# Splitting weights three pieces ahead of their products instead of two, in a two-block transformer kernel on one core

## The chip, the core and the metric

The kernel runs on one core of a Trainium2 chip. The core has TensorE (PE), which multiplies matrices into PSUM banks, VectorE (DVE), ScalarE (ACT), GpSimd (POOL) and SyncE (SP), which issues the DMAs of the weights here. Each engine works through its own list of instructions in order and waits on semaphores for the others. The metric is the device time of one execution in microseconds, as the median over runs.

## The reference

The input is 256 tokens of width 2048. Two blocks follow each other, all in float32.

```python
# block 1
h = rms_norm(x, pre_norm_w)
proj = h @ w_in                 # q, k, v, z, b, a of the delta rule; q, k, v, z of MoBA; two gates
oa = gated_delta_rule(conv+silu of q, k, v; beta, g)    # 8 heads of 128, chunks of 64
ob = moba_attention(qb, kb, vb)                          # 8 heads of 128, causal
merged = sigmoid(gate_a) * (norm(oa)*silu(z) @ w_branch_a) + sigmoid(gate_b) * (ob*silu(z) @ w_branch_b)
x = x + rms_norm(merged @ w_out, post_norm_w)
# block 2
proj = rms_norm(x, norm_g) @ w_in_2
# a: rope; compressed keys and values: silu(blocks @ cmp_w1) @ cmp_w2; compressed, selected
#    and window attention (8 heads of 128, 2 for keys), mixed by gates, times silu(za)
# b: rope; banded attention, window 128, with a sink per head (16 heads of 64, 2 for keys), times silu(zb)
x = x + concat(y_a, y_b) @ w_out_2
out = rms_norm(x, final_g)
```

## The kernel before

**Pieces and ticks.** All weights pass through the core once, as 398 pieces of 512 KB (fewer bytes for the pieces of kvb), in the order of the list `PIECES`. The program counts in ticks: tick n is the one in which TensorE multiplies piece n. The large products keep float32 accuracy by splitting both factors into a high and a low part; a piece takes part in three products, hi·hi, lo of the weight, and lo of the activations.

**What is done to a piece.** SyncE loads it into one of five raw slots (`load`, L772). ScalarE copies it, rounded, to a high part (`hi_w`, L973), VectorE subtracts this from the raw piece and writes the low part (`lo_w`, L1356). The two share one of four split slots. `split(no)` on ScalarE waits for the load of the piece and for the product of the piece that used the slot before, four full pieces earlier; on VectorE it waits for the high part. TensorE's `products(no)` (L2017 and others) waits for the low part. `load(no)` waits until the raw slot is free: for the lo_w of piece no-5.

**Pieces without a split.** The compression weights are multiplied raw (L1981, the "cmp" kind). They come in turns of two, pieces 276/277, 284/285, 292/293, 300/301, 308/309, 316/317, 324/325 and 332/333; `FULL` is the list of all other pieces. A load whose raw slot holds such a piece waits for TensorE's use of it in place of a lo_w. So load(c+5), with c the first piece of a turn, waits for the product of piece c.

**The order by hand.** `PLAN`, made by `plan()`, holds for each tick the small steps that run beside the products: on each of ScalarE and VectorE, the loop over ticks first splits the piece that `split_at(tick)` names, two full pieces ahead, and then runs the tick's steps. TensorE does the product of the tick first and then its steps. Around the border between the blocks (`BORDER` = 255, the last piece of w_out) `split_at` gives nothing and the splits stand in `PLAN`; also for the last piece (`FINAL` = 397).

**Steps that matter here.** A tile of attention, `att(kind, h, t, n)`, takes five ticks, one for each n: n = 0, the scores on TensorE; n = 1, mask and maximum on VectorE (L1614 to L1622); n = 2, exp on ScalarE (L1153); n = 3, transposes on TensorE (L1899) and then their copy `att_p` on ScalarE (L1163); n = 4, the product with the values on TensorE (L2253, L2260). Kind b is the banded attention, s the selected one; t = 0 and 1 are the halves of the tokens, of which the second has twice the keys. `rope(name, t)` on VectorE (L1744 to L1756) turns a projected group, `rope_flip` transposes it on TensorE (L1899). `cmp_fold` ends with a copy `hs_k` on ScalarE (L1259). `h2_hi` and `h2_lo` (ScalarE L1192, VectorE L1714) write the activations of block 2.

Of the kernel before, what the change touches and what calls it, by code (L numbers as in the profile page):

```python
# [46 lines left out]
PAIR = 64  # L47
RAW_SLOTS = 5
SPLIT_SLOTS = 4
AHEAD = 2  # L50
AUX = 4
NARROW, TABLES = 10, 20

# [108 lines left out]
TICKS = len(PIECES)  # L162
FULL = [_no for _no, _piece in enumerate(PIECES) if GROUPS[_piece[0]].kind != "cmp"]
# [4 lines left out]
BORDER = END[("wo", 3)]  # L168
FINAL = END[("w2", 3)]
# [6 lines left out]
def slot_of(no):  # L176

    return {1: SPLIT_SLOTS, 2: SPLIT_SLOTS + 1}.get(no - BORDER, FULL.index(no) % SPLIT_SLOTS)


def slot_before(no):

    return next((m for m in range(no - 1, -1, -1) if m in FULL and slot_of(m) == slot_of(no)), None)


def split_at(tick):

    if tick >= TICKS or tick not in FULL or tick == FINAL - 2 or -3 <= tick - BORDER <= 4:
        return None
    no = FULL[FULL.index(tick) + AHEAD]  # L190
    return no if no < TICKS else None

# [5 lines left out]
def plan():  # L200
    steps = [[] for _ in range(TICKS + LAST)]

    def at(tick, *step):
        steps[tick].append(step)
# [22 lines left out]
    for h in range(2):  # L227
        for part in "qkv":
            for n in range(2):
                c = END[("conv", part, h, n)]  # L230
# [59 lines left out]
    c = BORDER  # L290
# [34 lines left out]
    for t in range(NT):  # L325
        at(c + 4, "residual", 3, t)
    at(c + 4, "split", c + 6)
    at(c + 5, "sq2", 1)
    for t in range(NT):
        at(c + 5, "h2_flip", 3, t)  # L330
# [7 lines left out]
    def full(tick, n=0):  # L338

        return next(f for f in range(len(FULL)) if FULL[f] >= tick) + n  # L340
# [4 lines left out]
    def quiet(f):  # L345

        while f >= start and f not in free:
            f += 1
        return FULL[f]

    def attend(f, kind, h):
        for t in range(NT):
            for n in range(5):
                at(FULL[f + 4 * t + n], "att", kind, h, t, n)
            free.append(f + 4 * t + 2)
        return f + 4 * NT

    f = start
    for kind, h in (("b", 0), ("b", 1), ("b", 2), ("b", 3), ("s", 0), ("w", 0)):
        f = attend(f, kind, h)  # L360
# [3 lines left out]
    f = attend(attend(f + 5, "s", 1), "w", 1)  # L364
# [3 lines left out]
    for name in (("kcv",), ("kvb",), ("qb", 0), ("qb", 1), ("ksv",), ("qa", 0), ("kwv",), ("qa", 1)):  # L368
        c = full(END[name])
# [3 lines left out]
    for n, part in enumerate("kv"):  # L373
        at(FULL[full(END[("kcv",)]) + 5 + n], "blocks", part)
        c = full(END[("cmp", part)])
        at(FULL[c], "cmp_rows", part)
        c = full(quiet(c + 1))
# [3 lines left out]
    for m, name in enumerate((("zb", 0), ("zb", 1), ("za", 0), ("za", 1))):  # L381
        n = (m + 2) % 4
        c = full(END[name])
# [4 lines left out]
            at(quiet(gate + 1), "flip", "y", n, t)  # L388
    for c in range(3):
        at(END[("w2", c)] + 1, "y2_out", c)  # L390
    at(FINAL - 3, "split", FINAL)
    at(FINAL - 2, "tail", 0)
    at(FINAL, "tail", 1)

# [3 lines left out]


PLAN = plan()  # L400


# [27 lines left out]
def build(nc, known, ins, out):  # L430

    ctx = ExitStack()
    with ctx:
# [298 lines left out]
        def piece_source(no, col=None, cols=None):  # L732
            g, k0, n, _, _ = PIECES[no]
            group = GROUPS[g]
            w = ins[group.weight][0]
            col = group.col if col is None else col
            cols = group.cols if cols is None else cols
            return w[k0 * P:(k0 + n) * P, col:col + cols].rearrange("(k p) c -> p k c", p=P)

        def piece_view(buf, no):  # L740
            g, _, n, _, _ = PIECES[no]
            group = GROUPS[g]
            view = buf[:, 0:n * group.pitch].rearrange("p (k c) -> p k c", k=n)
            return view if group.pitch == group.cols else view[:, :, 0:group.cols]

        def piece_flat(buf, no):
            g, _, n, _, _ = PIECES[no]
            group = GROUPS[g]
            return buf[:, 0:n * group.cols] if group.pitch == group.cols else piece_view(buf, no)
# [209 lines left out]
        def _(act):  # L959
# [7 lines left out]
            def split(no):  # L967

                slot = slot_of(no)
                act.wait_ge(*raw_ready[no % RAW_SLOTS].after(no))  # L970
                if slot_before(no) is not None:
                    act.wait_ge(*used.after(slot_before(no)))
                act.activation(piece_flat(hi_w[slot], no), piece_flat(raw_w[no % RAW_SLOTS], no), ACT.Copy).then_inc(  # L973
                    *hi_ready.event(no))
# [358 lines left out]
                     "cmp_fold": cmp_fold, "cmp_out": cmp_out, "catt": catt,  # L1333
                     "z2_out": z2_out, "y2_out": y2_out, "tail": tail_}
            for tick in range(TICKS + LAST):
                if split_at(tick) is not None:
                    split(split_at(tick))
                for name, *args in PLAN[tick]:
                    if name in steps:
                        steps[name](*args)  # L1340
# [3 lines left out]
        def _(dve):  # L1344
# [7 lines left out]
            def split(no):  # L1352

                slot = slot_of(no)
                dve.wait_ge(*hi_ready.after(no))
                dve.tensor_tensor(piece_flat(lo_w[slot], no), piece_flat(raw_w[no % RAW_SLOTS], no),  # L1356
                                  piece_flat(hi_w[slot], no).bitcast(F32), ALU.subtract).then_inc(*lo_ready.event(no))
# [520 lines left out]
                     "norm2_col": norm2_col_, "rope_tables": rope_tables, "rope": rope,  # L1878
                     "blocks": blocks, "catt": catt, "y_gate": y_gate, "y2_out": y2_out, "tail": tail_}
            for tick in range(TICKS + LAST):  # L1880
                if split_at(tick) is not None:
                    split(split_at(tick))
                for name, *args in PLAN[tick]:
                    if name in steps:
                        steps[name](*args)
# [547 lines left out]
```

## Time and profile before

| | |
|---|---|
| median of 3 runs | 1208.56 us (1208.23 to 1208.69) |
| profiled execution | 1208.29 us, span 1206.5 us, mean granted clock 0.998 |
| TensorE busy | 1196.0 us, 99% of the span |
| TensorE weight loads | 996.6 us, 83% |
| VectorE busy | 753.8 us, 62% |
| ScalarE busy | 609.7 us, 51% |
| loads of raw pieces, issue to landing | 4.0 us in the median (w_in, w_in_2) |

The span is the time from the first instruction to the last on the core; 1.79 us of the execution lie around it. The chain that ended last is 96% TensorE. A releaser in the waits is the instruction that came last before the waiting one could start.

### The profile page before, as it was taken

What the parts mean: (1) busy time and instruction counts of PE and PEld (TensorE: products, weight loads), DVE (VectorE), ACT (ScalarE), POOL (GpSimd) and SP (SyncE); (2) the same over time, 40 slices, a digit from 0 to 9 for tenths busy, and PEclk for the clock granted to TensorE, in tenths of its full rate; (3) what the DMA queues carried; (4) which work ended last, traced back from release to release, by engine and by line L of the source; (5) the groups of instructions that cost most, each with busy time, mean ns of one, the idle gap of its engine ahead of it and who ended that gap; (6) DMA issues with size and microseconds to landing.
All of it is one profiled execution on the core that took longest, in us unless ns stands there. A gap on an engine that the chain in (4) does not pass through costs nothing.

```text
span 1206.5 us, 16121 instructions
## 1 busy us (share of the span) xinstructions
PE 1196.0 (99%) x6358; PEld 996.6 (83%) x6358; DVE 753.8 (62%) x1006; ACT 609.7 (51%) x899; POOL 98.4 (8%) x134
## 2 busy tenths in 40 slices
PE   9999999999999999999999999999999999999997
PEld 7888888888888888888888888888777778888886
DVE  5768786766665666555454454586665665676654
ACT  6656554454433456644444444474446547556443
POOL 0001010239710000000000000000000000000000
PEclk9999999999999999999999999999999999999999
DMA  8756565566654454565666676656746555454862
GB/s 287 227 155 205 171 189 160 162 191 194 195 152 136 126 169 143 174 193 175 205 183 196 197 285 201 199 183 196 240 158 233 168 173 187 129 157 143 297 198 95
DMA packets 145307, 224.03 MB, mean 186 GB/s; under 512 B 12176, under 2 KB 67152, under 8 KB 144208
## 3 DMA queue, kind: packets, MB, share of 16 engines
q1 hardware_dynamic: 142848, 212.50, 57.0%
q0 software_dynamic: 2064, 9.45, 2.2%
q8 instruction: 51, 0.84, 0.3%
q10 hardware_dynamic: 320, 1.06, 0.2%
q14 instruction: 24, 0.20, 0.0%
HBM read 218.25 MB, written 4.72 MB: 185 GB/s over the span
## 4 chain that ended last, share of the span: by engine, by line
PE 96%; ACT 1%; DVE 1%; DMA 1%; issue 0%; SPq 0%; POOLq 0%; POOL 0%; ACTq 0%; DVEq 0%
PE acc L2017 64%; PE acc L2007 12%; PE acc L2009 6%; PE aux L1899 3%; PE acc L1958 2%; PE aux L2232 1%; PE aux L2260 1%; PE aux L1981 1%; DMA raw_w<-in_w_in 1%; PE aux L2122 1%; PE aux L2225 1%; PE aux L2253 1%; ACT hi_w L973 1%; DVE lo_w L1356 0%; PE aux L2072 0%
## 5 line engine op out<-in xcount | busy, mean ns | idle before, releaser
L1356 DVE TENSOR_TENSOR lo_w<-raw_w,hi_w 128x1024 fp32r<-128x1024 f32 (+1 forms) x380 | 464.8, 1232 | 320.1 <-ACT hi_w L973 318.9
L973 ACT ACTIVATE hi_w<-raw_w 128x1024 fp32r<-128x1024 f32 (+1 forms) x380 | 394.1, 1053 | 275.5 <-PE acc L2017 173.6
L2017 PE MATMUL acc<-hi_w,h_both 128*128 128x512 f32 (+1 forms) x1616 | 519.4, 393 | 0.9 <-DVE h_both L1409 0.5
L2017 PEld LDWEIGHTS acc<-hi_w,h_both 128*128 128x128 f32 x1616 | 301.6, 188 | 66.8 <-issue 4.6
L2017 PE MATMUL acc<-lo_w,h_both 128*128 128x512 f32 (+1 forms) x808 | 312.0, 386 | 0.0
L2007 PE MATMUL acc<-h_both,hi_w 128*128 128x512 f32 x640 | 225.3, 397 | 0.0
L2009 PE MATMUL acc<-h_both,lo_w 128*128 128x256 f32 x640 | 178.5, 279 | 0.0
L2017 PEld LDWEIGHTS acc<-lo_w,h_both 128*128 128x128 f32 x808 | 152.0, 188 | 27.6
L2007 PEld LDWEIGHTS acc<-h_both,hi_w 128*128 128x128 f32 x640 | 120.1, 188 | 28.5
L2009 PEld LDWEIGHTS acc<-h_both,lo_w 128*128 128x128 f32 x640 | 120.5, 188 | 0.1
L2017 PE MATMUL acc<-hi_w,m_hi 128*128 128x512 f32 x224 | 87.7, 391 | 0.0
L2017 PE MATMUL acc<-hi_w,m_lo 128*128 128x512 f32 x224 | 87.2, 389 | 0.0
L2017 PE MATMUL acc<-lo_w,m_hi 128*128 128x512 f32 x224 | 87.2, 389 | 0.0
L2017 PEld LDWEIGHTS acc<-hi_w,m_lo 128*128 128x128 f32 x224 | 42.0, 188 | 8.8
L2017 PEld LDWEIGHTS acc<-lo_w,m_hi 128*128 128x128 f32 x224 | 42.1, 188 | 8.6
L2017 PEld LDWEIGHTS acc<-hi_w,m_hi 128*128 128x128 f32 x224 | 42.1, 188 | 8.6
L1153 ACT ACTIVATE att_s<-att_s,small 128x128 f32<-128x128 f32 (+1 forms) x80 | 35.3, 443 | 20.7 <-DVE small L1622 20.6
L1471 DVE SCALAR_TENSOR_TENSOR cv<-raw,conv_w,cv 128x255 f32<-128x255 f32 (+2 forms) x72 | 31.5, 479 | 1.0
L1163 ACT ACTIVATE att_p<-aux 128x512 f32<-128x512 f32 (+1 forms) x20 | 16.2, 812 | 31.0 <-PE aux L1899 31.0
L891 POOL TENSOR_TENSOR small_term<-small_block 64x31 f32<-64x31 f32 (+15 forms) x31 | 28.9, 932 | 2.4
L894 POOL TENSOR_TENSOR small_block<-small_block,small_term 64x31 f32<-64x31 f32 (+15 forms) x31 | 27.8, 897 | 2.4
L942 POOL DMA_DIRECT2D x<-x_scratch x1 | 0.8, 768 | 304.9 <-PE aux L2260 304.9
(356 smaller groups left out, 1148.3 us busy)
## 6 DMA issues: line engine op xcount, KB each, us to landing
raw_w<-in_w_in SPq DMA_DIRECT2D x279, 512.0 KB, 4.0
raw_w<-in_w_out SPq DMA_DIRECT2D x64, 512.0 KB, 4.5
raw_w<-in_w_branch_a SPq DMA_DIRECT2D x16, 512.0 KB, 4.8
raw_w<-in_w_branch_b SPq DMA_DIRECT2D x16, 512.0 KB, 4.8
raw_w<-in_cmp_k_w SPq DMA_DIRECT2D x8, 512.0 KB, 6.3
raw_w<-in_cmp_v_w SPq DMA_DIRECT2D x8, 512.0 KB, 6.7
x_in<-in_x SPq DMA_DIRECT2D x8, 256.0 KB, 7.2
x<-in_x POOLq DMA_DIRECT2D x1, 2048.0 KB, 9.4
```

The costliest lines, as they stand in the source:

```text
L891: link(pool.tensor_tensor(term, x[:, j + 1:BLOCK, j].unsqueeze(1).broadcast_to([n, rows, cols]), x[:, 0:rows, j].unsqueeze(2).broadcast_to ...
L894: last = pool.tensor_tensor(to, to, term, ALU.add)
L973: act.activation(piece_flat(hi_w[slot], no), piece_flat(raw_w[no % RAW_SLOTS], no), ACT.Copy).then_inc(*hi_ready.event(no))
L1153: e = act.activation(att_s[:, i * k:(i + 1) * k], att_s[:, i * k:(i + 1) * k], ACT.Exp, bias=nmx[:, i:i + 1], scale=sc, accum_out=den[:, i ...
L1163: act.activation(att_p[:, 0:t + 1], aux[:, b:b + t + 1], ACT.Copy).then_inc(*act_did.event("att_p", kind, h, t))
L1356: dve.tensor_tensor(piece_flat(lo_w[slot], no), piece_flat(raw_w[no % RAW_SLOTS], no), piece_flat(hi_w[slot], no).bitcast(F32), ALU.subtra ...
L1471: last = dve.scalar_tensor_tensor(cv[:, i, back:SEQ], raw[:, i, 0:SEQ - back], conv_w[:, CONV - 1 - back, first + i:first + i + 1], cv[:, ...
L1899: return pe.transpose(to, source, ident[0:source.shape[0], 0:source.shape[0]])
L1958: i = pe.matmul(acc[:, g_ % 2, t], x[at], w[:, k], start=first and k == 0 and m == 0, stop=(no, t) in HALF_ENDS and k == n - 1 and m == 2)
L2007: pe.matmul(to[:, c].rearrange("p (b c) -> p b c", b=2), hi[:, k, cols], x, start=first and k == 0, stop=False)
L2009: i = pe.matmul(to[:, c, 0:SEQ], lo[:, k, cols], x[:, 0], start=False, stop=last and k == n - 1)
L2017: i = pe.matmul(to[:, t, 0:group.cols], x[at], w[:, k], start=first and k == 0 and m == 0, stop=last and k == n - 1 and m == 2)
```

## The change

`AHEAD` goes from 2 to 3. `split_at` becomes `splits_at` and returns a list: two pieces ahead below tick 9, both two and three ahead at tick 9, three ahead from there on. It gives nothing for the ticks 251 to 259 (before: 252 to 259). In `PLAN`, tick 260 splits piece 262, and the split of the last piece is no longer there, since `splits_at` names it. The loops on ScalarE and VectorE go over the list. Nothing else changes: slots, loads, products and steps are the same.

```diff
--- before.py
+++ after.py
@@ -47,7 +47,7 @@
 PAIR = 64
 RAW_SLOTS = 5
 SPLIT_SLOTS = 4
-AHEAD = 2
+EARLY_AHEAD, AHEAD, CATCH_UP = 2, 3, 9
 AUX = 4
 NARROW, TABLES = 10, 20
 
@@ -183,12 +183,13 @@
     return next((m for m in range(no - 1, -1, -1) if m in FULL and slot_of(m) == slot_of(no)), None)
 
 
-def split_at(tick):
-
-    if tick >= TICKS or tick not in FULL or tick == FINAL - 2 or -3 <= tick - BORDER <= 4:
-        return None
-    no = FULL[FULL.index(tick) + AHEAD]
-    return no if no < TICKS else None
+def splits_at(tick):
+
+    if tick >= TICKS or tick not in FULL or -4 <= tick - BORDER <= 4:
+        return []
+    f = FULL.index(tick)
+    ahead = (EARLY_AHEAD,) if tick < CATCH_UP else (EARLY_AHEAD, AHEAD) if tick == CATCH_UP else (AHEAD,)
+    return [FULL[f + a] for a in ahead if FULL[f + a] < TICKS]
 
 
 
@@ -325,6 +326,7 @@
     for t in range(NT):
         at(c + 4, "residual", 3, t)
     at(c + 4, "split", c + 6)
+    at(c + 5, "split", c + 7)
     at(c + 5, "sq2", 1)
     for t in range(NT):
         at(c + 5, "h2_flip", 3, t)
@@ -388,7 +390,6 @@
             at(quiet(gate + 1), "flip", "y", n, t)
     for c in range(3):
         at(END[("w2", c)] + 1, "y2_out", c)
-    at(FINAL - 3, "split", FINAL)
     at(FINAL - 2, "tail", 0)
     at(FINAL, "tail", 1)
 
@@ -1333,8 +1334,8 @@
                      "cmp_fold": cmp_fold, "cmp_out": cmp_out, "catt": catt,
                      "z2_out": z2_out, "y2_out": y2_out, "tail": tail_}
             for tick in range(TICKS + LAST):
-                if split_at(tick) is not None:
-                    split(split_at(tick))
+                for no in splits_at(tick):
+                    split(no)
                 for name, *args in PLAN[tick]:
                     if name in steps:
                         steps[name](*args)
@@ -1878,8 +1879,8 @@
                      "norm2_col": norm2_col_, "rope_tables": rope_tables, "rope": rope,
                      "blocks": blocks, "catt": catt, "y_gate": y_gate, "y2_out": y2_out, "tail": tail_}
             for tick in range(TICKS + LAST):
-                if split_at(tick) is not None:
-                    split(split_at(tick))
+                for no in splits_at(tick):
+                    split(no)
                 for name, *args in PLAN[tick]:
                     if name in steps:
                         steps[name](*args)
```

In the lists below a name such as raw_w0 is raw slot 0 (piece number modulo 5), and line numbers after the change are one higher.

VectorE at tick 302, in the turn of pieces 300 and 301, before. After the lo_w of piece 304 come n = 1 of the attention (b1, second half), the first half of ksv's rope, and then raw_w0, piece 305:

```order
L1639 COPY ob_t_164<-aux 128x2x128
L1356 TENSOR_TENSOR lo_w0_58<-raw_w4_53,hi_w0_54 128x1024
L1614 TENSOR_TENSOR att_s_130<-aux,masks_67 128x2x2x256
L1617 TENSOR_REDUCE small_74<-att_s_130 128x4
L1620 SCALAR_TENSOR_TENSOR small_74<-small_74 128x4
L1621 TENSOR_TENSOR small_74<-small_74 128x4
L1622 TENSOR_SCALAR small_74<-small_74 128x4
L1744 TENSOR_TENSOR rot0_172<-acc,rope_a_70 128x256
L1745 TENSOR_TENSOR rot1_173<-acc,rope_a_70 128x2x64
L1746 TENSOR_TENSOR rot1_173<-acc,rope_a_70 128x2x64
L1756 TENSOR_TENSOR rot2_174<-rot0_172,rot1_173 128x256
L1356 TENSOR_TENSOR lo_w1_59<-raw_w0_49,hi_w1_55 128x1024
```

The same place in the changed kernel:

```order
L1640 COPY ob_t_164<-aux 128x2x128
L1357 TENSOR_TENSOR lo_w1_59<-raw_w0_49,hi_w1_55 128x1024
L1615 TENSOR_TENSOR att_s_130<-aux,masks_67 128x2x2x256
L1618 TENSOR_REDUCE small_74<-att_s_130 128x4
L1621 SCALAR_TENSOR_TENSOR small_74<-small_74 128x4
L1622 TENSOR_TENSOR small_74<-small_74 128x4
L1623 TENSOR_SCALAR small_74<-small_74 128x4
L1745 TENSOR_TENSOR rot0_172<-acc,rope_a_70 128x256
L1746 TENSOR_TENSOR rot1_173<-acc,rope_a_70 128x2x64
L1747 TENSOR_TENSOR rot1_173<-acc,rope_a_70 128x2x64
L1757 TENSOR_TENSOR rot2_174<-rot0_172,rot1_173 128x256
```

The lo_w of piece 305 has moved from between the two halves of the rope to a place ahead of the attention's n = 1.

ScalarE at ticks 303 and 304 before; raw_w1 is piece 306 and raw_w2 piece 307:

```order
L1151 ACTIVATE small_74<-small_74 128x4
L1153 ACTIVATE att_s_130,small_74<-att_s_130,small_74 128x256 x4
L1230 ACTIVATE vs_tok_154<-acc,small_74 128x256 x2
L1259 ACT_TABLE_LOAD
L1259 ACTIVATE hs_k_158<-aux 128x128
L973 ACTIVATE hi_w2_56<-raw_w1_50 128x1024
L1163 ACTIVATE att_p_131<-aux 128x1024
L973 ACTIVATE hi_w3_57<-raw_w2_51 128x1024
```

The same steps in the changed kernel:

```order
L974 ACTIVATE hi_w2_56<-raw_w1_50 128x1024
L1152 ACTIVATE small_74<-small_74 128x4
L1154 ACTIVATE att_s_130,small_74<-att_s_130,small_74 128x256 x4
L1231 ACTIVATE vs_tok_154<-acc,small_74 128x256 x2
L1260 ACT_TABLE_LOAD
L1260 ACTIVATE hs_k_158<-aux 128x128
L974 ACTIVATE hi_w3_57<-raw_w2_51 128x1024
L1164 ACTIVATE att_p_131<-aux 128x1024
```

The hi_w of 306 now stands ahead of the exp, and that of 307 between hs_k and att_p.

VectorE at ticks 280 and 281 before, the rope of qb 0; raw_w2 is here piece 282 and raw_w3 piece 283:

```order
L1356 TENSOR_TENSOR lo_w0_58<-raw_w2_51,hi_w0_54 128x1024
L1744 TENSOR_TENSOR rot0_172<-acc,rope_b_71 128x512
L1745 TENSOR_TENSOR rot1_173<-acc,rope_b_71 128x8x32
L1746 TENSOR_TENSOR rot1_173<-acc,rope_b_71 128x8x32
L1756 TENSOR_TENSOR rot2_174<-rot0_172,rot1_173 128x512
L1356 TENSOR_TENSOR lo_w1_59<-raw_w3_52,hi_w1_55 128x1024
L1744 TENSOR_TENSOR rot0_172<-acc,rope_b_71 128x512
L1745 TENSOR_TENSOR rot1_173<-acc,rope_b_71 128x8x32
L1746 TENSOR_TENSOR rot1_173<-acc,rope_b_71 128x8x32
L1756 TENSOR_TENSOR rot2_174<-rot0_172,rot1_173 128x512
```

In the changed kernel, where raw_w3 is piece 283 and raw_w1 piece 286:

```order
L1357 TENSOR_TENSOR lo_w1_59<-raw_w3_52,hi_w1_55 128x1024
L1745 TENSOR_TENSOR rot0_172<-acc,rope_b_71 128x512
L1746 TENSOR_TENSOR rot1_173<-acc,rope_b_71 128x8x32
L1747 TENSOR_TENSOR rot1_173<-acc,rope_b_71 128x8x32
L1757 TENSOR_TENSOR rot2_174<-rot0_172,rot1_173 128x512
L1357 TENSOR_TENSOR lo_w2_60<-raw_w1_50,hi_w2_56 128x1024
L1745 TENSOR_TENSOR rot0_172<-acc,rope_b_71 128x512
L1746 TENSOR_TENSOR rot1_173<-acc,rope_b_71 128x8x32
L1747 TENSOR_TENSOR rot1_173<-acc,rope_b_71 128x8x32
L1757 TENSOR_TENSOR rot2_174<-rot0_172,rot1_173 128x512
```

Between the halves of the rope stands the lo_w of 286 in place of that of 283.

## Rows read from the trace of the kernel before

**Rows 1.** The page, part 1: busy us, share of the span, instructions.

```profile
PE 1196.0 (99%) x6358; PEld 996.6 (83%) x6358; DVE 753.8 (62%) x1006; ACT 609.7 (51%) x899; POOL 98.4 (8%) x134
```

**Rows 2.** Waits of TensorE: us in total, times, longest us.

```profile
PE acc L2359 <- POOL ones L839: 1.1, 1, 1.1
...
```

**Rows 3.** Waits of ScalarE, the same columns.

```profile
...
ACT hi_w L973 <- DMA raw_w<-in_w_in: 37.4, 20, 5.7
...
```

**Rows 4.** Timelines at the border: start us, duration us, engine, line, operation, [idle before].

```profile
801.13 2.15 DVE L1714 SCALAR_TENSOR_TENSOR h_both<-aux,norm_col,h_both 128x128 fp32r<-128x128 f32 x8
...
803.03 0.47 PE L2017 MATMUL acc<-hi_w,h_both 128*128 128x512 f32 x1 [0.32 <-DVE h_both L1714]
...
805.86 1.03 DVE L1356 TENSOR_TENSOR lo_w<-raw_w,hi_w 128x840 fp32r<-128x840 f32 x1 [2.58 <-ACT hi_w L973]
```

**Rows 5.** Timelines at kvb's rope, VectorE and TensorE.

```profile
819.18 1.23 DVE L1356 TENSOR_TENSOR lo_w<-raw_w,hi_w 128x1024 fp32r<-128x1024 f32 x1 [0.20 <-ACT hi_w L973]
...
829.24 0.49 DVE L1754 TENSOR_TENSOR rot<-rot,rot 128x128 f32<-128x128 f32 x2
...
829.91 0.60 PE L1899 MATMUL aux<-ident,rot 128*128 128x128 f32 x4
```

**Rows 6.** Timelines at the rope of qb 0.

```profile
849.46 1.22 DVE L1356 TENSOR_TENSOR lo_w<-raw_w,hi_w 128x1024 fp32r<-128x1024 f32 x1
...
850.78 1.06 ACT L973 ACTIVATE hi_w<-raw_w 128x1024 fp32r<-128x1024 f32 x1 [3.04 <-DMA raw_w<-in_w_in]
...
851.97 0.69 DVE L1756 TENSOR_TENSOR rot<-rot,rot 128x512 f32<-128x512 f32 x1
...
853.43 1.04 PE L1899 MATMUL aux<-ident,rot 128*128 128x128 f32 x8
```

**Rows 7.** Timelines of the turn at piece 300.

```profile
901.85 1.39 SPq L772 DMA_DIRECT2D raw_w<-in_w_in  x3
...
905.42 1.06 ACT L973 ACTIVATE hi_w<-raw_w 128x1024 fp32r<-128x1024 f32 x1 [2.76 <-DMA raw_w<-in_w_in]
...
906.39 0.19 ACT L1151 ACTIVATE small<-small 128x4 f32<-128x4 f32 x1
...
906.52 1.23 DVE L1356 TENSOR_TENSOR lo_w<-raw_w,hi_w 128x1024 fp32r<-128x1024 f32 x1 [0.65 <-ACT hi_w L973]
...
908.50 0.84 ACT L1230 ACTIVATE vs_tok<-acc,small 128x256 f32<-128x256 f32 x2
...
909.36 1.28 ACT L1259 ACT_TABLE_LOAD   x1
...
910.98 1.03 PE L1899 MATMUL aux<-ident,att_s 128*128 128x128 f32 x8
...
912.05 1.03 ACT L1163 ACTIVATE att_p<-aux 128x1024 f32<-128x1024 f32 x1 [0.17 <-PE aux L1899]
...
914.68 0.65 PE L2253 MATMUL aux<-att_p,vb 128*64 128x256 f32 x4
```

**Rows 8.** Windows, VectorE, one attention tile's n = 1: window, length and busy us.

```profile
858.79:860.66 1.87, 1.77 (x6) 1.00 0.57 113
901.74:904.69 2.95, 2.85 (x7) 1.00 0.60 162
```

**Rows 9.** Timelines of the turns at pieces 284, 316 and 332.

```profile
863.23 1.22 DVE L1356 TENSOR_TENSOR lo_w<-raw_w,hi_w 128x1024 fp32r<-128x1024 f32 x1 [2.57 <-ACT hi_w L973]
...
867.09 0.60 PE L1899 MATMUL aux<-ident,att_s 128*128 128x128 f32 x4
...
950.83 1.22 DVE L1356 TENSOR_TENSOR lo_w<-raw_w,hi_w 128x1024 fp32r<-128x1024 f32 x1 [2.56 <-ACT hi_w L973]
...
951.98 1.03 PE L1899 MATMUL aux<-ident,rot 128*128 128x128 f32 x8
...
996.19 1.23 DVE L1356 TENSOR_TENSOR lo_w<-raw_w,hi_w 128x1024 fp32r<-128x1024 f32 x1 [0.90 <-ACT hi_w L973]
...
1000.24 1.03 PE L1899 MATMUL aux<-ident,att_s 128*128 128x128 f32 x8
```

## The prediction, made before the changed kernel ran

> **What bounds the kernel now.** I read the page first. TensorE is busy for 99% of the span [rows 1], so time can only be won where TensorE waits, and it is lost wherever a change makes TensorE wait. The view of TensorE's waits has four rows, the longest 1.1 us for a constant at the start [rows 2], and none of the four is for a hi_w or lo_w. No product waits for a split. So splitting a piece one tick earlier has nothing to remove: its gain is bounded by zero, give or take a tenth.
>
> The next view is the waits of ScalarE. Its splits wait 20 times, 37.4 us in all, for the DMA that brings the raw weights [rows 3]. That happens behind the pieces that go to TensorE raw (the two-piece turns of the compression weights, ticks 276 to 333): load(c+5) may be issued only when TensorE has used raw piece c. For c = 300 it is issued at 901.85 and the split starts on its landing at 905.42 [rows 7]. This wait is free now because little stands behind it.
>
> **What the change does.** The number of splits and loads stays; only the places change. From tick 9 on, split(s) of a tick stands at the head of ScalarE's and VectorE's lists as before, but is that of one piece later. So every other step of these two engines has one more split in front of it: one hi_w on ScalarE and one lo_w of 1.22 us on VectorE. In ordinary ticks I cost this at nothing: the two splits of a tick take 1.06 and 1.23 us on two engines, while TensorE takes 3.7 us from one tick's small work to the next one's (910.98 to 914.68) [rows 7], and attention hands a tile over only once in two ticks. If that cover were missing, each miss would cost up to 1.2 us. The last split before the end, the start, and ticks 252 to 259 keep their order. What remains are the places where TensorE waits closely for a step of VectorE or ScalarE. I went through the timelines tick by tick for those.
>
> *Border, tick 261.* The narrow lo_w of piece 264 (1.03 us) now stands before the last h2_lo, which began at 801.13; product 262 started at 803.03 after waiting 0.32 us for it [rows 4]. Pieces 262 and 263 change places, which ends the two some 0.3 us earlier. Cost 1.03 - 0.3 = **0.7 us** (0.3 to 1.1).
>
> *Rope of kvb, ticks 270 to 272.* VectorE runs without a gap from 819.18 to 829.73, and TensorE's transposes start at 829.91, 0.2 us later [rows 5]. One more lo_w of 1.22 us enters this chain, and the chain can begin some 0.5 us earlier, since a small lo_w before it moves into idle time: 1.22 - 0.5 - 0.2 = **0.6 us** (0 to 1.1).
>
> *Rope of qb 0.* lo_w of 283 ran after the first half (849.46 to 850.68), the rope's second half then took until 852.66, 2.0 us, and the transposes started at 853.43. Now lo_w of 286 stands before the second half, and its raw piece lands only at 850.78 (ScalarE waited 3.04 us for that DMA) [rows 6]: hi_w to 851.84, lo_w to 853.1, rope to 855.1, transposes at 855.2: **1.75 us** (1.2 to 2.3).
>
> *The turns.* split(c+5) stood at tick c+3; now it stands at c+2, where the data has not landed. Both queues stop for it. On VectorE the masks and the maximum of an attention tile (n = 1) stand behind, ScalarE's exp waits for these, and TensorE's transposes (n = 3) for the exp. Before, n = 1 ran inside the wait.
> - c = 300 (b1, second half). lo_w of 305 ends at 907.75 [rows 7]. Then n = 1, 2.95 us [rows 8], to 910.65; exp, 2.1 us (906.39 to the start of vs_tok at 908.50), to 912.8. TensorE stood ready at 910.98 [rows 7]: **+1.85** (1.5 to 2.3). Behind it on VectorE the rope of ksv is pushed too (1.3 us, lo_w of 306 1.2 us, the second half until 913.7); vs_tok waits for that (0.84), then a table load (1.28), hs_k (0.3) and, new in front of att_p, hi_w of 307 (1.05): att_p runs 917.0 to 918.0. TensorE wants it at 914.68 [rows 7] + 1.85 = 916.5: **+1.5** (0 to 2).
> - c = 284 (b0, first half). lo_w of 289 ends at 864.45 [rows 9]; n = 1, 1.87 us [rows 8], to 866.3; exp of half the width about 1.7 (estimate from the 2.1 above), to 868.0; TensorE was there at 867.09 [rows 9]: **+1.0** (0.5 to 1.5).
> - c = 316 (b3, first half). lo_w of 321 ends at 952.05 [rows 9]; n = 1 as narrow, to 953.9. Here TensorE's transposes of the rope reuse the bank that n = 1 reads; they started at 951.98 [rows 9]: **+1.95** (1 to 2.4).
> - c = 332 (s0, second half). lo_w of 337 ends at 997.42 [rows 9]; n = 1 without the sink's small operations about 2.7 (below the 2.95 of [rows 8]), exp 2.1, to 1002.2; TensorE was there at 1000.24 [rows 9]: **+1.9** (1.4 to 2.3).
> - c = 292, 308, 324: what stands behind the wait there is att_p, about 1 us, of which TensorE leaves 0.6 us or more after the delay: 0 (0 to 0.8 each).
>
> A delay of TensorE moves the release of the next raw slot with it, so the terms add up.
>
> The Trainium skill's "DMA: Bandwidth & Descriptors", section "Rules for kernel authors", says to issue a DMA early, compute, and wait on its semaphore late. The turns show that rule in their own numbers: the 3.5 us from issue to landing were filled with n = 1, and the change puts the wait ahead of it. By that rule the change loses in the turns, as the sum has it.
>
> **The sum** is 0.7 + 0.6 + 1.75 + 1.85 + 1.5 + 1.0 + 1.95 + 1.9 = 11.25 us. The profiled execution took 1208.29 us (span 1206.5 and 1.79 around it); it lies 0.27 us below the median of 1208.56. So 1219.5 in the profile's terms, 1219.8 against the median. I predict 1219.7 us. The low ends together give 5.9 (1214.4), the high ends 17.4 (1226).
>
> **Rivals.**
> 1. *Part of it is swallowed.* The two indirect terms (att_p at c = 300, the bank at c = 316) and those at the border and kvb rest on slacks of a few tenths that I chained. Without them: 1.75 + 1.85 + 1.0 + 1.9 = 6.5, 1215.1 us. For it: each rests on several steps. Against it: the rows are dense there, and each list is strictly in order.
> 2. *More waits than I found.* Every turn costs (three more of about 0.8), and some ordinary ticks, where the new hi_w waits for the slot that the product just before gives back, push an exp by up to 1 us: 11.25 + 2.4 + about 2, 1224.2 us. For it: 16 attention tiles in block 2 and 4 in block 1, all behind such splits now. Against: two whole products lie between n = 1 and n = 3.
> 3. *Not slower: the loads come earlier too.* A load waits for the lo_w of five pieces before. If lo_w is made a tick earlier, its successor is issued up to 2.7 us earlier, and the data would be there when the earlier split asks for it; the 37.4 us of [rows 3] would move with the work, and TensorE keeps its 99%: 1208.3 to 1208.6, no change. It decides the matter if the load of c+5 also depends on a split. Against: that load waits for TensorE's use of piece c (901.85 in [rows 7] follows the raw product), which no split moves. The same rival in its best form, a gain of the border's 0.3 us and the like, ends at 1208.0.
> 4. *The change does not do what it says:* the slot gate (the product of four pieces before) holds ScalarE's splits to their old times, and nothing behind them is late. In plain stretches that is so already; in the turns the DMA, not the slot, is the gate, so there it can't be. Same time as rival 3.
>
> **Chances.** Forecast, 1217 to 1222: 0.5. Rival 1, down to 1213: 0.22. Rival 2, up to 1226: 0.14. Rivals 3 and 4: 0.11, with 0.02 of it faster. A still smaller loss, between 1211 and 1213, takes the last 0.03. What this kernel's measurement can tell from no change is about 0.2%, 2.4 us. Faster 0.02, same 0.09, slower 0.89. The range that holds 8 in 10 is 1213 to 1225; the forecast's own is 1217 to 1222.
>
> **What would show it.** In the changed kernel's profile TensorE's busy time stays at 1196.0 and the rest of the span rises from 10.5 to some 22 us. Its waits list DVE small (n = 1) or ACT att_s (exp) before the transposes, some 1 to 2 us each at 868, 912, 954 and 1002 (shifted by what was lost before), an ACT att_p of 1.5 us near 918, DVE rot of 1.75 at 855 and 0.6 at 830, and 0.7 more of DVE h_both at 803. The DMA waits of ScalarE's splits grow. Up to 795 us the two traces agree within 0.3 us. I am wrong if time is lost in block 1, if the turns show no wait of TensorE, or if the waits for att_p and at c = 292, 308, 324 change places in size.

## The result, and the profile after

| | before | after |
|---|---|---|
| median | 1208.39 us (1208.23 to 1208.69, 4 runs) | 1221.36 us (1220.34 to 1226.87, 4 runs) |
| ratio | | 1.0116, 95% interval 1.0093 to 1.0139 |
| profiled execution | 1208.29 us, span 1206.5 | 1220.34 us, span 1218.5 |
| TensorE busy | 1196.0 us | 1197.3 us |

The change makes the kernel slower by 1.2%. The same program in a later comparison gave 1221.03 us (1220.73 to 1221.66, 4 runs), ratio 1.0102 (1.0087 to 1.0118).

The page after shows it in two lines. TensorE has almost the same work [rows 1], and its share of the chain fell from 96% to 90%; VectorE, the DMA and ScalarE stand in the gap:

```profile
PE 1197.3 (98%) x6358; PEld 996.3 (82%) x6358; DVE 754.9 (62%) x1006; ACT 614.0 (50%) x899; POOL 99.8 (8%) x134
PE 90%; DVE 4%; DMA 3%; ACT 2%; issue 1%; SPq 0%; POOLq 0%; POOL 0%; ACTq 0%; DVEq 0%
```

The waits of TensorE after (us in total, times, longest). Of [rows 2] only the constant at the start was of any size before:

```profile
PE aux L1900 <- ACT att_s L1154: 5.0, 3, 1.9
PE aux L1900 <- DVE small L1623: 2.0, 1, 2.0
PE aux L1900 <- DVE rot L1757: 1.8, 1, 1.8
PE acc L2360 <- POOL ones L840: 1.2, 1, 1.2
PE acc L2018 <- DVE h_both L1715: 1.1, 1, 1.1
PE aux L1900 <- DVE rot L1755: 0.6, 1, 0.6
...
```

And where they stand, in TensorE's timeline after (start, duration, line, operation, idle before it and what ended it). In order these answer to the TensorE rows of [rows 4], [rows 5], [rows 6], then 867.09 of [rows 9], 910.98 of [rows 7], 951.98 and 1000.24 of [rows 9]:

```profile
802.97 0.47 PE L2018 MATMUL acc<-hi_w,h_both 128*128 128x512 f32 x1 [1.06 <-DVE h_both L1715]
...
830.62 0.63 PE L1900 MATMUL aux<-ident,rot 128*128 128x128 f32 x4 [0.64 <-DVE rot L1755]
...
856.10 0.63 PE L1900 MATMUL aux<-ident,rot 128*128 128x128 f32 x4 [1.81 <-DVE rot L1757]
...
871.18 0.63 PE L1900 MATMUL aux<-ident,att_s 128*128 128x128 f32 x4 [1.22 <-ACT att_s L1154]
...
917.20 0.60 PE L1900 MATMUL aux<-ident,att_s 128*128 128x128 f32 x3 [1.95 <-ACT att_s L1154]
...
961.97 0.41 PE L1900 MATMUL aux<-ident,rot 128*128 128x128 f32 x2 [1.99 <-DVE small L1623]
...
1012.22 0.52 PE L1900 MATMUL aux<-ident,att_s 128*128 128x128 f32 x3 [1.79 <-ACT att_s L1154]
```

Seven waits, each where the sum had a term; its eighth term, att_p at c = 300, has no wait here. Less the 0.32 us that the first already had, they make 10.14 us. I set the start of each of TensorE's 6358 matmuls against its start before. At 795 us TensorE is 0.8 us ahead of before, at the end 12.0 behind, so it loses 12.8 us in between: the 10.14 us of waits, another 1.7 us between 917 and 922 us without waiting, and 1.0 us at the seven waits beyond their idle time. Nearly all of this last part is 0.16 us at each of the six waits of transposes: without a wait the first transpose starts 0.16 us before the end that the profile gives to the matmul ahead of it (in the trace of before at 910.98, behind one of 910.75 that is 0.39 long), behind a wait it does not. For the 1.7 us the windows of TensorE after show why (window, length, busy, granted clock in the fourth number, DMA share, GB/s):

```profile
914.00:917.00 3.00, 1.25 (x6) 1.00 0.57 215
917.00:918.00 1.00, 0.80 (x5) 0.75 0.00 0
918.00:919.00 1.00, 1.00 (x6) 0.50 0.76 123
919.00:920.00 1.00, 1.00 (x4) 0.50 0.98 360
920.00:921.00 1.00, 1.00 (x4) 0.54 0.15 55
921.00:922.00 1.00, 1.00 (x6) 1.00 0.01 2
```

TensorE stood still for 1.95 us up to 917.20, and then ran at half the clock (1.2 of 2.4 GHz) for about 3 us. The mechanism ahead of the 917 wait begins with the load of piece 305. It is issued 4.12 us later than before (901.85 in [rows 7]), which is just how far TensorE is behind by then, so the earlier split has not brought it forward; hi_w waits for it:

```profile
905.97 1.39 SPq L773 DMA_DIRECT2D raw_w<-in_w_in  x3
...
909.67 1.06 ACT L974 ACTIVATE hi_w<-raw_w 128x1024 fp32r<-128x1024 f32 x1 [7.17 <-DMA raw_w<-in_w_in]
```

VectorE's timeline after goes on from there, beside the lo_w of [rows 7]: the lo_w of piece 305 waits for the raw load through its hi_w, and n = 1 of the attention stands behind it. Before, n = 1 started at 901.74 [rows 8], ahead of that lo_w.

```profile
910.76 1.23 DVE L1357 TENSOR_TENSOR lo_w<-raw_w,hi_w 128x1024 fp32r<-128x1024 f32 x1 [5.95 <-ACT hi_w L974]
911.90 1.22 DVE L1615 TENSOR_TENSOR att_s<-aux,masks 128x1024 f32<-128x1024 f32 x1
```

The DMA waits of ScalarE's splits grew from the 37.4 us of [rows 3] to 57.4:

```profile
ACT hi_w L974 <- DMA raw_w<-in_w_in: 57.4, 21, 8.3
```

### The profile page after: what moved, and what is told of

Same layout as the page of the kernel before. It is cut to its first block, busy times and chain, and to the rows that moved or that the text cites. A ratio compares the mean times of both kernels' runs of the same rounds, so it can differ in the third digit from the quotient of the medians.

```text
span 1218.5 us, 16121 instructions
## 1 busy us (share of the span) xinstructions
PE 1197.3 (98%) x6358; PEld 996.3 (82%) x6358; DVE 754.9 (62%) x1006; ACT 614.0 (50%) x899; POOL 99.8 (8%) x134
## 3 DMA queue, kind: packets, MB, share of 16 engines
q10 hardware_dynamic: 320, 1.06, 0.2%
## 4 chain that ended last, share of the span: by engine, by line
PE 90%; DVE 4%; DMA 3%; ACT 2%; issue 1%; SPq 0%; POOLq 0%; POOL 0%; ACTq 0%; DVEq 0%
PE acc L2018 59%; PE acc L2008 12%; PE acc L2010 6%; PE aux L1900 4%; DMA raw_w<-in_w_in 3%; PE acc L1959 2%; PE aux L2233 1%; PE aux L2261 1%; DVE lo_w L1357 1%; ACT hi_w L974 1%; PE aux L2123 1%; PE aux L2226 1%; PE aux L2254 1%; PE aux L1982 0%; DVE h_both L1715 0%
## 5 line engine op out<-in xcount | busy, mean ns | idle before, releaser
L974 ACT ACTIVATE hi_w<-raw_w 128x1024 fp32r<-128x1024 f32 (+1 forms) x380 | 399.7, 1055 | 446.6 <-PE acc L2018 284.7
L2018 PE MATMUL acc<-hi_w,oa_hi 128*128 128x512 f32 x64 | 25.0, 390 | 0.0
```

Of the source, the lines that this page charges most:

```text
L2018: i = pe.matmul(to[:, t, 0:group.cols], x[at], w[:, k], start=first and k == 0 and m == 0, stop=last and k == n - 1 and m == 2)
```

## Experiments

All kernels but the repeated one have this in place of the changed kernel's `splits_at`; `before_at` and `after_at` are the two orders, and `MOVED` moves single splits. Where block 2 is as before, the two lines of `PLAN` that the change touched (piece 262 at tick 260, the last piece) are as before too:

```diff
+FIRST_AHEAD = True     # block 1 three ahead (False: as before)
+SECOND_AHEAD = True    # block 2 three ahead (False: as before)
+MOVED = {}             # piece: tick at whose head it is split instead
+def splits_at(tick):
+    ahead = FIRST_AHEAD if tick <= BORDER - 4 else SECOND_AHEAD
+    own = after_at(tick) if ahead else before_at(tick)
+    return sorted([no for no in own if no not in MOVED] + [no for no in MOVED if MOVED[no] == tick])
```

### Each block alone

Theory: a handful of places in block 2 where a late step meets a close TensorE. Rivals: something spread over all ticks, or block 1.

```diff
 FIRST_AHEAD = True
-SECOND_AHEAD = True
+SECOND_AHEAD = False
```

> The change up to the border only (three ahead for ticks 9 to 250), block 2 as before. Theory (the loss is a handful of waits in block 2): no wait of TensorE over 0.1 us beyond those of before, and 1207.6 us, 0.8 less than before, since the trace of the changed kernel stood 0.8 us earlier than that of before at 795 us. Rival A (that 0.8 us is scatter from one execution to the next): 1208.4 us, within 0.3. Rival B (part of the loss arises in block 1 and shows only later): over 1209.5 us.

Measured: 1208.86 us (1207.61 to 1211.49, 11 runs) against 1208.73, ratio 1.0 (0.9991 to 1.0009). Block 1 is no part of the loss that the median shows; nor did the 0.8 us that I hoped for show in it, and the executions spread over 3.9 us. Its trace has three small new waits, which the experiment on the triangular step below explains. It has others above the 0.1 us that I had allowed: 0.28 us for `inv` at 342 us, and 0.15 and 0.41 us in the first 10 us.

```diff
-FIRST_AHEAD = True
+FIRST_AHEAD = False
 SECOND_AHEAD = True
```

> The change after the border only; block 1 as before. Theory: all seven waits of TensorE stay (0.7 more at 803, 0.6 at 830, 1.8 at 855, 1.2 at 870, 1.9 at 917, 2.0 at 961, 1.8 at 1011) and with them the whole loss: 1220 to 1222 us. Rival B: under 1218 us.

Measured: 1221.73 us (1220.53 to 1223.01, 4 runs), ratio 1.0108 (1.0094 to 1.0121). All seven waits are there, and the whole loss. One thing is different, and it is the term that the first trace had hidden. Here the clock stayed up behind the 917 wait, and a wait for att_p appears, as TensorE's timeline shows:

```profile
917.97 1.06 PE L1920 MATMUL aux<-ident,att_s 128*128 128x128 f32 x8 [1.86 <-ACT att_s L1174]
...
923.08 0.65 PE L2274 MATMUL aux<-att_p,vb 128*64 128x256 f32 x4 [1.30 <-ACT att_p L1184]
```

ScalarE's timeline of the same kernel has the queue in front of att_p, in the order that the prediction had worked out:

```profile
918.70 0.84 ACT L1251 ACTIVATE vs_tok<-acc,small 128x256 f32<-128x256 f32 x2 [0.87 <-DVE rot L1767]
919.55 1.28 ACT L1280 ACT_TABLE_LOAD   x1
920.85 0.28 ACT L1280 ACTIVATE hs_k<-aux 128x128 f32<-128x128 f32 x1
921.02 1.05 ACT L994 ACTIVATE hi_w<-raw_w 128x1024 fp32r<-128x1024 f32 x1
921.97 1.02 ACT L1184 ACTIVATE att_p<-aux 128x1024 f32<-128x1024 f32 x1
```

So att_p is 1.3 us late at full clock. In the first trace att_p came as long after the transposes began (4.0 us in both), but at half clock the transposes and the product behind them took 1.7 us longer and hid that wait: at this place the two prices are alternatives, not a sum.

### The turns put back

```diff
-MOVED = {}
+MOVED = {c + 5: c + 3 for c in (276, 284, 292, 300, 308, 316, 324, 332)}
```

> The changed kernel, but the split of the first piece after each raw turn (281, 289, 297, 305, 313, 321, 329, 337) is asked for one tick later, as before the change; all other splits stay three ahead. Theory (the wait for the raw load has come ahead of the attention's steps): the four waits at 870, 917, 961 and 1011 are gone, and with them the slow stretch of TensorE's clock after the one at 917; what stays is border, kvb's rope and qb 0's rope, 3.2 us: 1211 us (1210.3 to 1211.7). Rival C (it is the number of splits ahead of the attention's steps, not the load): the four waits stay at over 1 us, 1219 us or more.

Measured: 1214.79 us (1211.95 to 1215.23, 5 runs), ratio 1.0044 (1.0031 to 1.0056). Three of the four turn waits are gone. A wait of 0.5 us for the exp stays near 873: besides the split after the turn, that of 290 stands before the exp too, and with the table load it ends the exp late. The expected 1211 us was missed by 3.8 us, 3.1 beyond the high end, and the trace (1215.23 us) has more reasons than that wait. TensorE was 0.8 us behind before at 800 us. The wait for qb 0's rope grew to 2.16 us, and this time the half clock came with that one, as TensorE's windows show:

```profile
857.00:858.00 1.00, 0.00 (x0) 0.97 0.00 0
858.00:859.00 1.00, 0.94 (x5) 0.50 0.00 0
859.00:860.00 1.00, 1.00 (x6) 0.50 0.00 0
860.00:861.00 1.00, 1.00 (x4) 0.50 0.00 0
861.00:862.00 1.00, 1.00 (x5) 0.82 0.00 0
```

### Border and ropes put back, and then all of it

```diff
-MOVED = {}
+MOVED = {263: 261, 264: 262, 274: 272, 286: 282}
```

> The changed kernel with four splits asked for as before the change: 263 at tick 261 and 264 at tick 262 (border), 274 at tick 272 (rope of kvb), 286 at tick 282 (rope of qb 0). The turns stay as changed. Theory (each wait comes from the one split ahead of the late step): the extra waits at 803 (0.7), 830 (0.6) and 855 (1.8) are gone, the four of the turns stay (1.2, 1.9, 2.0, 1.8) and what follows the one at 917 (1.3 to 1.7): 1217.5 us (1216.5 to 1219). Rival (the lead as a whole, not the four splits): 1220.5 us or more.

Measured: 1215.73 us (1215.58 to 1217.85, 5 runs), ratio 1.0064 (1.0051 to 1.0076), 0.8 us under the low end that I gave. The waits at 803, 830 and 855 are back at or below what they were, so each of these three comes from what was put back ahead of its late step: one split at each rope, two together at the border. The turns remain, one of them smaller (0.94 instead of 1.22):

```profile
PE aux L1920 <- ACT att_s L1174: 4.4, 3, 1.8
PE aux L1920 <- DVE small L1643: 1.9, 1, 1.9
PE aux L2274 <- ACT att_p L1184: 1.3, 1, 1.3
```

```diff
-MOVED = {}
+MOVED = {263: 261, 264: 262, 274: 272, 286: 282, **{c + 5: c + 3 for c in (276, 284, ..., 332)}}
```

> The changed kernel with those four splits and the eight first ones after the raw turns (281, 289, 297, 305, 313, 321, 329, 337) asked for as before the change. All others, some 350, stay three ahead. Theory: no wait over 0.4 us is added; 1208.8 us, within 0.6 of before (block 1 adds three of 0.25 us). Rival (something spread over all ticks costs too, and was hidden in the sum): 1210.5 us or more. Wait for the exp near 870: it was 0.5 us with the eight put back alone and may stay.

Measured: 1208.74 us (1207.74 to 1209.96, 11 runs) against 1208.37, ratio 1.0003 (0.9994 to 1.0012). Twelve of 380 splits together carry all of the loss that the median can tell, which is to about 1 us. Waits of 0.59 us at 853 and 0.32 us at 867 are left in the trace, and TensorE loses 1.3 us at these two places; it had reached them 0.9 us earlier than before, since the stretch up to 335 us was the shorter one in this trace (see the last section). So the other splits three ahead bring nothing that shows, and a small cost of theirs in block 2 isn't excluded.

### One split alone

The kernel before with one split moved:

```diff
-MOVED = {}
+MOVED = {305: 302}
```

> The kernel before, with one split moved: piece 305 at tick 302 instead of 303. Theory: one wait of TensorE of 1.85 us before the transposes near 911, and behind it either a wait for att_p of up to 1.5 us or a slow stretch of the clock of that length: 1210.3 to 1212.0 us. Prediction's form (att_p late by itself because hi_w of 307 and the rope stand before it): here hi_w of 307 is behind att_p again, so without the clock the second part is 0.4 us or less, 1210.3 to 1210.8. Rival C (one split does nothing): 1208.4 us.

Measured: 1211.41 us (1210.33 to 1212.73, 11 runs), ratio 1.0021 (1.0012 to 1.003). One split one tick earlier costs 2.7 us of the 12. The trace, of an execution of 1212.02 us, has the wait and half the clock behind it, worth 1.6 us, as TensorE's timeline and windows show. The executions spread over 2.4 us.

```profile
913.06 1.58 PE L1920 MATMUL aux<-ident,att_s 128*128 128x128 f32 x8 [1.92 <-ACT att_s L1174]
...
913.00:914.00 1.00, 0.94 (x6) 0.72 0.06 16
914.00:915.00 1.00, 1.00 (x5) 0.50 0.00 0
915.00:916.00 1.00, 1.00 (x4) 0.50 0.00 0
916.00:917.00 1.00, 1.00 (x4) 0.57 0.00 0
```

### Is it the standing still that lowers the clock?

```diff
 # TensorE, n = 3 of tile b1, second half; the destination banks are free, the exp is not done
+                    if (kind, h, t) == ("b", 1, 1):
+                        for m in range(16):
+                            o = m % QUAD * P
+                            turn(aux[:, att_bank(kind) + m // 8, o:o + P], ident[:])
                     pe.wait_ge(*act_did.after("exp", kind, h, t))
```

> The kernel before with piece 305 split at tick 302 (the wait of 1.9 us before the transposes near 911), and 16 transposes of the constant ident put into that wait, whose results are overwritten. They need no data and TensorE would stand still there otherwise. Theory (after the wait TensorE's clock is at its lower level for some 3 us in part of the executions, because TensorE stood still): with the gap filled the clock stays at its upper level, and the 1.9 us of the wait are the whole cost: 1210.6 us, all runs within 0.7 of each other. Rival (the clock drops for another reason): as without the filling, 1211.4 us with runs from 1210.3 to 1212.7.

Measured: 1210.78 us (1210.16 to 1211.42, 11 runs), ratio 1.0019 (1.001 to 1.0028). The slow tail is gone: the slowest execution is 1.3 us faster than the slowest without the filling, and the spread is 1.3 us instead of 2.4, where I had expected all within 0.7 of each other. The median is 0.6 lower, but the two kernels ran on different chips; against before on its own chip it is 2.41 us instead of 2.68, only 0.3 less. In the trace the clock stays up:

```profile
912.35 1.09 PE L1920 MATMUL aux<-ident,att_s 128*128 128x128 f32 x8
...
913.00:917.00 4.00, 3.63 (x21) 1.00 0.00 0
```

Three things keep this from being proof. The two intervals overlap. The clock stayed up behind most of the unfilled waits too, so one trace says little. And the filling saves time whatever the clock does: the late exp pushes the transposes by 2.08 us without it and by 1.79 with it, and these 0.3 us are the whole difference of the medians. Only the missing tail speaks for the clock; I call the theory supported, not shown.

```diff
-MOVED = {305: 302}
+MOVED = {305: 302, 306: 303, 307: 304}
```

> As the one before, with pieces 306 and 307 asked for one tick earlier too (ticks 303 and 304), so that hi_w of 307 stands before att_p as in the changed kernel. Theory (the prediction's att_p term is real and is only hidden when the clock is low): a wait for att_p of 1.3 us appears near 918: 1211.9 us (1211.5 to 1212.3). Rival (att_p is late only because everything is): no such wait, 1210.6 us.

Measured: 1211.52 us (1211.06 to 1211.87, 9 runs), ratio 1.0025 (1.0015 to 1.0035), and in the trace the wait:

```profile
PE aux L2278 <- ACT att_p L1184: 1.3, 1, 1.3
```

With hi_w of 307 ahead of att_p the wait for att_p is 1.34 us; with it behind, as in the filled kernel before this one, it is 0.37. In the medians the difference is 0.7 us where 1.0 was due.

### The changed kernel again

> The changed kernel again, unaltered, for more executions beside those of before on one chip. 1220.3 to 1224 us. For the clock theory (after a wait of some 2 us TensorE's clock is low for 3 us in part of the executions) the executions should scatter over more than 2 us, those of before over less than 2. For the stretch from 256 to 335 us, in which four of the five traces with block 1 three ahead are 1.5 us shorter than all with two ahead: 78.8 or 80.3 us, nothing between.

Measured: 1221.03 us (1220.73 to 1221.66, 4 runs). The scatter that I expected did not come in these four: 0.9 us, less than the 1.8 of before on that chip. In its trace the half clock came behind the wait at 856 (1.7 us lost there), the 918 wait was followed by full clock, and att_p was late by 1.28 us. The stretch from 256 to 335 us was the shorter one.

### The triangular step, and two waits of before

Three ahead also put a lo_w in front of the triangular step of the delta rule (L1508 to L1516 before), which TensorE awaits:

```diff
-SECOND_AHEAD = True
-MOVED = {}
+SECOND_AHEAD = False
+MOVED = {69: 67, 73: 71, 77: 75, 81: 79}
```

> Block 1 three ahead as in the changed kernel, block 2 as before the change, and the four splits that the change put ahead of the triangular step of the delta rule (69, 73, 77, 81) one tick later, behind it. Theory (the three new waits of 0.08 us at 227, 241 and 255, each with 0.25 us of delay, and the old one of 0.32 at 213 come from the lo_w in front of this step): all four are gone, 0.75 us less than block 1 alone, 1208.0 us, at best 1207.3. Rival: the step waits for something else, 1208.7 us as with block 1 alone.

Measured: 1207.67 us (1207.35 to 1208.28, 11 runs) against 1208.44 us, ratio 0.9993 (0.9984 to 1.0001). All four waits are gone, TensorE's waits are down to

```profile
PE acc L2380 <- POOL ones L860: 1.2, 1, 1.2
PE acc L2038 <- DVE h_both L1430: 0.6, 1, 0.6
PE acc L2038 <- DVE h_both L1735: 0.3, 1, 0.3
PE aux L2215 <- issue: 0.2, 1, 0.2
```

and its median is the lowest here, 0.8 us below before, though the interval includes 1.

```diff
-FIRST_AHEAD, SECOND_AHEAD = True, True
+FIRST_AHEAD, SECOND_AHEAD = False, False
-MOVED = {}
+MOVED = {68: 67, 263: 262}
```

> The kernel before with two splits one tick later: 68 at tick 67 instead of 66 (it stood ahead of the triangular step, before which TensorE waited 0.32 us at 213) and 263 at tick 262 instead of 261 (ahead of h2_hi and h2_lo, 0.32 us at 803). Theory: both waits go, 0.6 to 1.0 us less than before: 1207.6 us. Rival (something else ends these waits, the splits do not): within 0.2 of before.

Measured: 1209.39 us (1209.04 to 1210.13, 11 runs), ratio 1.0008 (0.9999 to 1.0016), slower where I expected faster. Both waits went (at 213, and at 803: the matmul of 803.03 in [rows 4] came 1.1 us earlier), and a new one took their place:

```profile
PE acc L2038 <- DVE lo_w L1377: 1.8, 1, 1.8
```

By moving 263 to tick 262 I had put it behind the four squares (L985, 3 us) of tick 261 on ScalarE, which I had not counted: hi_w of 263 started only at 804.10, and its product, due at 804.8, ran from 806.56.

```diff
-FIRST_AHEAD, SECOND_AHEAD = True, True
+FIRST_AHEAD, SECOND_AHEAD = True, False
-MOVED = {}
+MOVED = {69: 67, 73: 71, 77: 75, 81: 79, 263: 262}
```

> Block 1 three ahead with 69, 73, 77 and 81 behind the triangular step, block 2 as before the change but with 263 at tick 262. All that the runs have pointed to in one kernel: 1207.3 us (1206 to 1208), the fastest of all, if the gains of the two others add up; if three ahead in block 1 brings nothing of its own, the same as the kernel with two splits moved.

Measured: 1209.2 us (1208.91 to 1209.46, 11 runs), ratio 1.0005 (0.9996 to 1.0014). The same mistake, and the same wait of 1.75 us at 806. Without 263 it would be the kernel of 1207.67.

## Why the prediction was right, by its own steps

Forecast 1219.7, measured 1221.36; the profiled execution has 1220.34 where the sum had 1219.5. The mechanism, a step or a rope pushed behind a split, was right at every place that it named. That the total came so close is in part luck. The waits alone are 10.14 us where the sum without att_p has 9.75. Half clock (1.7) stood in for att_p (1.5). The 1.0 us that TensorE lost beyond the idle time of its waits was in no term, nor were the 0.8 us that it was ahead at 795, and these two nearly cancel. TensorE's busy time rose by 1.3 us, to 1197.3, where 1196.0 was said: the half clock and the 1.0 us add to it, and the stretch up to 335 us, 1.5 us shorter, takes from it.

- **Nothing to gain** at the products: right. With the twelve put back and all others three ahead the time is that of before.
- **Border** 0.7: 0.74 (1.06 less 0.32). **kvb** 0.6: 0.64. **qb 0** 1.75: 1.81. The repair shows that they hang on the splits put back, one at each rope and two together at the border.
- **c = 300, exp** 1.85: 1.95, and 1.92 with that split alone. **att_p** 1.5: 1.28 to 1.30 in the three traces with this order whose clock was up there (block 2 alone, ropes put back, the changed kernel again) and 1.34 with the gap filled. In the first trace it was 0, because the half clock took 1.7 in its place. The step was right in its mechanism, but the prediction had no clock in it.
- **c = 284** 1.0: 1.22, and the exp waited last for n = 1, as said. Hi_w of 290 and a table load, which the sum left out, stand before the exp too: ScalarE stood idle for 0.53 us behind them, until n = 1 was done. They are what held the exp for 0.5 us once the turn's split was put back.
- **c = 316** 1.95: 1.99, released by `small` as said, through the bank and not through the exp. **c = 332** 1.9: 1.79.
- **c = 292, 308, 324** 0: no wait.
- **Slips in the working**: 907.75 + 2.95 is 910.7, not 910.65; the chain before att_p adds up to 917.2, not 917.0; c = 284 gives 0.9 and c = 332 gives 2.0 from the times shown; and 1208.56 + 5.9 is 1214.5. None moves the sum by more than 0.2 us.
- **Block 1 costed at nothing**: wrong in its parts. Three waits of 0.08 to 0.09 us before the transposes of the triangular step push TensorE by 0.26 us each, 0.8 us in all, and time lost in block 1 was one of my own signs of being wrong. I had looked for attention steps, and there a lo_w stands before a step whose input comes just in time. Against that, in the traces of the changed kernel the stretch up to 335 us is 1.5 us shorter, so I missed the line "up to 795 within 0.3 us" by 0.5.
- **Rival 3** (loads come earlier too) fell for the reason given: the load of c+5 follows TensorE, as its issue at 905.97 shows, and ScalarE's DMA waits went up to 57.4 us. **Rival 2**: no trace of the changed kernel has its extra waits in the turns. Two of the first four executions were above the forecast's 1222, though. The slowest, 1226.87 us, had a mean granted clock of 0.994 against 0.997 in the profiled one; that is worth some 3 to 4 us of the 6.5 between them (an estimate, 0.003 of the time), and with no trace of it the rest stays open. **Rival 1** did not hold: all the small terms came, att_p where the clock was up.

## What to carry to other kernels

On an engine that works strictly through its list, as ScalarE and VectorE do here, moving prefetch work earlier moves its wait earlier, and all small steps behind it pay: before moving it, see which instruction of the moved kind waits for a transfer that something else must release, and what is queued behind. Nearly all of the cost lies where a step and its reader are close, here at seven waits behind 12 of 380 splits, so one lead for all ticks is too coarse. A move to the end of a list of steps needs the same look as one to the front: I paid 1.75 us for four squares that I had not counted.

## What the runs showed of the hardware

**The clock behind a wait.** Eight traces hold 19 waits of TensorE of 1.6 us or more. At four of them (1.88, 1.92, 1.95 and 2.16 us) the granted clock went to 0.50, between 0.1 us before the wait's end and 0.4 us after it, for about 3 us, which cost 1.6 to 1.7 us; at the 15 others, of 1.64 to 2.11 us, it stayed at 1.00. The Trainium skill, "TensorE: Matmul & The Clock Gate", Part 1, has the clock fall when the engine idles. The traces agree so far: apart from the end of each trace, 2 to 5 us after TensorE's last matmul, it fell only at such a wait. Which of two alike waits it follows they do not tell.

**Two paces at the same clock.** In the stretch of 455 matmuls from about 255 to 335 us, the granted clock is 1.00 in every trace, and yet it takes either 80.32 to 80.33 us (nine traces) or 78.81 us (five), never anything between; a 128x512 matmul has 399 or 393 ns there in the mean. All five shorter ones have block 1 three ahead with the triangular waits, but one such kernel (the turns put back) had the longer one, though its block 1 is the same program. What sets it stays open: no run here changed one thing about it.
